# A hybrid decoder step on one core: the sample's attention moved out of the opening into the second half of layer 0

## The reference, cut to what matters

```python
# layer 0 (even)
hp, hs = rms_norm(xp, norm_mix[0]), rms_norm(xs, norm_mix[0])
gate_b, gate_c, xv, q, k, v = split_projection(h, w_in)        # 6 x 512 columns
y_a = gated_short_conv(gate_b, gate_c * xv, conv_w)
# sample: every new token reads its own sequence's cache (8 x 1024 rows of keys
# and of values) at three (window, dilation) pairs, and itself
y_b = combine_branches([dilated_branch_sample(q, k_all, v_all, w, d, wb)
                        for w, d in ((128, 1), (512, 4), (2048, 16))])
x = x + concat([y_a, y_b]) @ w_out
# layer 1 (odd): x = x + pool_mix(rms_norm(x))
# every layer, after its mixer, for prompt and sample:
h = rms_norm(x); q = h @ wq                                    # 8 heads x 2 x 128
expert = top16(top16(q1 @ keys1) + top16(q2 @ keys2))          # of 128 x 128 experts
x = x + sum((softmax(cs) * gelu(h . u_tab[expert])) * v_tab[expert])
```

## Time and profile before

| | us |
|---|---|
| median of three runs | 3018.01 |
| the profiled execution: its own time | 3018.12 |
| its span in the trace | 3016.3 |
| PE busy in the span | 2627.3 (87%) |
| DVE busy | 2088.8 (69%) |
| ACT busy | 1289.9 (43%) |
| POOL busy | 1200.5 (40%) |
| moved by DMA | 1214.94 MB, mean 403 GB/s |
| HBM read / written | 1208.47 MB / 38.37 MB |

### The profile page before, as it was taken

The page is one execution under the profiler, slowest core; times in us unless marked ns, Lnnn a source line. Parts: engine busy times, 40 slices in busy tenths (PEclk is TensorE's granted clock), DMA queues, the critical chain, the costliest instruction groups (busy, mean ns, idle before and its releaser), DMA issues.

```text
span 3016.3 us, 27708 instructions
## 1 busy us (share of the span) xinstructions
PE 2627.3 (87%) x7481; PEld 1297.1 (43%) x7481; DVE 2088.8 (69%) x5117; ACT 1289.9 (43%) x3717; POOL 1200.5 (40%) x1104
## 2 busy tenths in 40 slices
PE   7989999999998887888898988878999977777787
PEld 6665565555544443333444434323444422222222
DVE  3547666787766667777667677777676767677666
ACT  2113445665444344444443444345443444444444
POOL 2103344343444444444444344444434543344442
PEclk9999999999999998999999999999999999999999
DMA  9869999999999999999999999999999999999997
GB/s 353 302 244 371 417 419 416 421 390 395 420 421 422 421 421 391 421 421 404 421 421 421 394 405 422 421 421 389 421 420 420 420 421 414 418 418 415 416 418 325
DMA packets 174472, 1214.94 MB, mean 403 GB/s; under 512 B 19714, under 2 KB 20238, under 8 KB 32613
## 3 DMA queue, kind: packets, MB, share of 16 engines
q0 software_dynamic: 155904, 1124.11, 90.4%
q1 hardware_dynamic: 18413, 89.07, 7.6%
HBM read 1208.47 MB, written 38.37 MB: 413 GB/s over the span
## 4 chain that ended last, share of the span: by engine, by line
DMA 44%; PE 38%; DVE 7%; ACT 6%; issue 3%; POOL 1%; DVEq 0%; SPq 0%; ACTq 0%; POOLq 0%
DMA RING<-in_peer_uv,idx 44%; PE PSUM L1171 24%; PE PSUM L882 10%; DVE RING L1770 4%; ACT diag L1342 2%; ACT L1338 1%; ACT gate L1339 1%; POOL RING L833 1%; PE PSUM L864 1%; ACT L1318 1%; ACT act_h L1338 1%; DVE H L1384 1%; PE PSUM L1162 1%; DMA RING<-in_peer_uv,pidx 1%; PE PSUM L894 0%
## 5 line engine op out<-in xcount | busy, mean ns | idle before, releaser
L1171 PE MATMUL PSUM<-RING,diag 128*128 128x512 f32 (+1 forms) x4160 | 1995.3, 616 | 344.5 <-ACT diag L1342 341.0
L833 POOL DMA_INDIRECT RING<-in_peer_uv,idx x1024 | 1147.7, 1121 | 1610.3 <-PE PSUM L1171 1505.6
L1770 DVE CUSTOM_DVE_ANT_0 RING<-RING,H 128x1024 f32<-128x1024 f32 x1032 | 1264.5, 1226 | 708.1 <-DMA RING<-in_peer_uv,idx 700.2
L1171 PEld LDWEIGHTS PSUM<-RING,diag 128*128 128x128 f32 (+1 forms) x4160 | 750.6, 191 | 1426.5 <-ACT diag L1342 785.1
L1338 ACT ACTIVATE act_h<-dots 128x1 f32<-128x1 f32 x1040 | 207.8, 200 | 1063.1 <-DVE dots L1770 1061.3
L1342 ACT ACTIVATE diag<-ident,gate 128x128 f32<-128x128 f32 x1024 | 411.2, 402 | 39.8 <-PE PSUM L1171 6.6
L882 PE MATMUL PSUM<-HT,WCH 128*128 128x256 f32 (+1 forms) x1536 | 366.4, 384 | 1.3 <-ACT HT L1216 1.3
L882 PEld LDWEIGHTS PSUM<-HT,WCH 128*128 128x128 f32 x1536 | 288.9, 191 | 98.9 <-issue 63.7
L1339 ACT ACTIVATE gate<-act_h,ex 128x1 f32<-128x1 f32 x1024 | 301.6, 294 | 33.2
L1338 ACT ACT_TABLE_LOAD x92 | 118.0, 1283 | 7.6 <-DVE dots L1770 6.0
L1216 ACT ACTIVATE YT<-PSUM 128x264 f32<-128x264 f32 (+2 forms) x68 | 27.0, 398 | 178.0 <-PE PSUM L882 172.4
(11 more groups left out here) (220 smaller groups left out, 1463.4 us busy)
## 6 DMA issues: line engine op xcount, KB each, us to landing
WCH<-in_peer_wq SPq DMA_DIRECT2D x32, 1024.0 KB, 9.2
WCH<-in_w_in_ab SPq DMA_DIRECT2D x18, 1024.0 KB, 9.6
RING<-in_peer_uv,idx POOLq DMA_INDIRECT x1024, 15.0
out_win_k_sample<-in_state_win_k POOLq DMA_DIRECT2D x8, 2016.0 KB, 12.3
out_win_v_sample<-in_state_win_v POOLq DMA_DIRECT2D x8, 2016.0 KB, 10.8
RING<-in_w_in_ab SPq DMA_DIRECT2D x6, 1024.0 KB, 10.9
WCH<-in_w_out_ab SPq DMA_DIRECT2D x6, 1024.0 KB, 9.4
X<-in_x_prompt SPq DMA_DIRECT2D x4, 512.0 KB, 14.8
```

The source lines that it names most:

```text
L833: pool.indirect_dma_start(rows[:, use % SLOTS, :], None, peer_uv.rearrange("l e n -> (l e) n"), bass.IndirectOffsetOnAxis(ap=at, axis=0),) ...
L1171: last = nc.tensor.matmul(PSUM[0:out_n, accumulator(n) + half, :], diag[:, use % DIAGS, 0:out_n], rows[:, use % SLOTS, D + half * 512:D + ...
L1770: V.tensor_tensor_reduce(out=u, in0=u, in1=row, scale=1.0, scalar=0.0, op0=ALU.mult, op1=ALU.add, accum_out=dots[:, tau % SETS, k:k + 1]). ...
```

## The change

The sample's attention, its residual add, its second norm and its queries leave the first half of layer 0 and go to the second. Its projections and its convolution stay in the opening; what is needed later (its query, value and convolution rows) is kept in SBUF tiles that live on.

- `has_sample` is now true for b = 1 in both layers, so the sample's column block rides with `wo`, `wt`, norm 3 and the queries of the second half (264 columns there, 256 in the first).
- The sample's pieces are laid over the second half by position (`sample_pieces`, `threaded`): a sequence's keys every 5 units of width, the softmax, a sequence's values every 4 units. The widths of that half sum to 187 instead of 166, over the same rows 40 to 204. The last four projection chunks go to the attention's steps 13 to 16 instead of 8 to 11.
- Keys and values now come through two buffers, the tile G and the first 1024 columns of YT, not four in RING; keys are multiplied in place. With the space won in RING the opening's weight pairs get seven homes instead of four.
- The value sums are turned round: for each sequence eight matmuls with 128 x 128 value rows as weights and 2 columns moving, into bank 4, instead of two with 512 columns moving; four more bring in the token's own value. `masked` and `gather_heads` go; two copies take their place.
- Jobs use the banks 0 to 3 from the second half on (`cut`), not 0 to 4.
- The last five cache copies start at `wo` chunks 0, 2, 4, 6, 7 of the opening. The expert keys are loaded at `own`, the second half's x rows at `tails`.

```diff
-NW_FIRST = 4
+NW_FIRST = 7
...
-NKV = 4
+NKV = 2
+OWN = 64
+SAMPLE_BANK = 4
...
-NORMS = ((1, 2, 0), (1, 2, 0), (3, 4), (3, 4), (1, 2), (1, 2), (3, 4, 0), (3, 4, 0), (1,), (2,), (3,), (4,), (0,))
+NORMS = ((1, 2, 0), (1, 2), (3, 4), (3, 4, 0), (1, 2), (1, 2), (3, 4, 0), (3, 4, 0), (1,), (2,), (3,), (4,), (0,))
...
 def has_sample(l, b):
-    return (l, b) in ((0, 0), (1, 1))
+    return b == 1
...
+KEYS_AT, KEY_STEP = 14, 5
+SCORED_AT = KEYS_AT + B * KEY_STEP + 1
+WEIGHED_AT = SCORED_AT + 5
+SPREAD_AT = WEIGHED_AT + 7
+SUMS_AT, SUM_STEP = SPREAD_AT + 7, 4
+
+def sample_pieces():
+
+    out = [(6, ("kv", n), 0) for n in range(NKV)]
+    for b in range(B):
+        at = KEYS_AT + b * KEY_STEP
+        out.extend([(at, ("qrep", b), 1), (at + KEY_STEP - 0.5, ("kv", NKV + b), 0)])
+    out.extend([(SCORED_AT, ("scored_sample",), 1), (WEIGHED_AT, ("weighed",), 0), (SPREAD_AT, ("weights",), 1)])
+    for b in range(B):
+        at = SUMS_AT + b * SUM_STEP
+        out.append((at, ("so", b), 1))
+        if B + NKV + b < 2 * B:
+            out.append((at + 1, ("kv", B + NKV + b), 0))
+    out.append((SUMS_AT + (B - 1) * SUM_STEP + 2, ("gathered",), 0))
+    return out
...
-        gated = [("p", b, kind, c) for kind in "cxb" for c in range(CA)]
+        gated = [("p", b, kind, c) for kind in "cx" for c in range(CA)]
+        gated += [None] * (BT * NH + 1 - 3 * CA) + [("p", b, "b", c) for c in range(CA)]
...
+        out = threaded(out, sample_pieces())
...
-    cut = names.index(("hT", 3, 0, 0))
+    cut = names.index(("gain", 2, 0))
...
+        kv = [rows.rearrange("p (t n) -> p t n", t=2) for rows in (G[:, :], YTf[:, 0:2 * DA])]
...
-                    + [("so", 2), ("so", 5), ("so", 7), ("wo", 0, 1), ("wo", 0, 4)])
+                    + [("wo", 0, c) for c in (0, 2, 4, 6, 7)])
...
             def sample_output(b):
...
+                    for c in range(CA):
+                        nc.tensor.matmul(out[:, c, :, :], v_row[:, c * P:(c + 1) * P], own_mix[:, c, :, :],
+                                         start=(c == 0), stop=False, skip_group_check=True)
                 pe.wait_ge(kv_loaded[n % NKV], 48 * (n // NKV + 1))
-                for c in range(2):
-                    last = nc.tensor.matmul(PSUM[0:B * NH, 7, :], SPT[:, c, b, :], kv[:, n % NKV, c, :],
-                                            start=(b == 0 and c == 0), stop=(b == B - 1 and c == 1))
+                for c in range(CA):
+                    heads = slice(b * NH + 2 * c, b * NH + 2 * c + 2)
+                    for t in range(2):
+                        last = nc.tensor.matmul(out[:, c, b, :], kv[n % NKV][:, t, c * P:(c + 1) * P], SPT[:, t, heads],
+                                                start=False, stop=(t == 1), skip_group_check=True)
                 last.then_inc(so_done, 1)
```

More of the change, by code:

```diff
@@ L87, in has_sample, with threaded @@
 def has_sample(l, b):
-    return (l, b) in ((0, 0), (1, 1))
+    return b == 1
 REPEATED = ((1, 0), (1, 1))
-OUTPUTS_AT = {9: (0,), 10: (1, 2), 11: (3, 4), 12: (5,), 13: (6,), 14: (7,)}
+KEYS_AT, KEY_STEP = 14, 5
[16 more added lines that the diff above has]
+    return out
+def threaded(main, among):
+    out, at, left = [], 0.0, sorted(among, key=lambda entry: entry[0])
+    for piece, n in main:
+        while left and left[0][0] <= at:
+            out.append(left.pop(0)[1:])
+        out.append((piece, n))
+        at += n
+    assert not left
+    return out
 def whole_pieces(l, b):
@@ L136, in whole_pieces @@
             if m == 8:
-                out.append((("scored_sample",), 1))
                 out.append((("tails", b), 1))
@@ L141, in whole_pieces @@
             out.append((("count", b, m + 1), 0.9))
-            if m < 8:
-                out.append((("qrep", m), 1))
-            elif m == 8:
-                out.append((("weighed",), 0))
-            else:
-                if m == 9:
-                    out.append((("weights",), 1))
-                for n in OUTPUTS_AT.get(m, ()):
-                    out.append((("so", n), 1))
-                if m == BT * NH - 1:
-                    out.append((("masked",), 1))
-                if m == BT * NH:
-                    out.append((("gathered",), 1))
         for c in range(KD):
@@ L157, in whole_pieces @@
             if c in (4, KD - 1):
-                for j in (*range(BT), "s"):
+                for j in range(BT):
                     out.append((("wt", b, j, c // 7), 1))
@@ L183, in whole_pieces @@
                 out.append((("wt", b, j, half), 1))
-            if b == 0:
-                out.append((("wt", b, "s", half), 1))
+            out.append((("wt", b, "s", half), 1))
+        out = threaded(out, sample_pieces())
     else:
@@ L483, in build @@
         o += 2 * CA * B
-        times = RING[0:B * NH, o:o + NS]
-        o += NS
         own_scores = RING[0:B, o:o + NH]
         o += NH
-        own_column = RING[0:B, o:o + B * NH]
-        o += B * NH
-        by_sample = RING[0:B * NH, o:o + B]
-        o += B
-        own_probs = RING[0:B * NH, o:o + NH]
-        o += NH
         assert o <= SLOTS * ROW
+        sel = X[OWN:OWN + B, 0, :].rearrange("p (b n) -> p b n", b=B)
+        q_row, v_row = (H[OWN:OWN + B, n * DA:(n + 1) * DA] for n in range(2))
         UW = BN + 2
@@ L531, in build @@
         o += NS
+        times = SC[0:B * NH, o:o + NS]
+        o += NS
+        own_column = SC[0:B, o:o + B * NH]
+        own_mix = SC[OWN:OWN + B, o:o + B * NH].rearrange("p (c b h) -> p c b h", c=CA, b=B)
+        o += B * NH
+        by_sample = SC[0:B * NH, o:o + B]
+        o += B
+        own_probs = SC[0:B * NH, o:o + NH]
+        o += NH
+        SPT = SC[:, o:o + 2 * B * NH].rearrange("p (t n) -> p t n", t=2)
+        o += 2 * B * NH
+        ys_kept = SC[:, o:o + CA * B].rearrange("p (c b) -> p c b", c=CA)
+        o += CA * B
         assert o <= T * HC * NK
```

149 lines of the change are left out of this document (58 added, 91 removed).

## The result

| | before | changed |
|---|---|---|
| median of the runs, us | 3018.5 (3016.9 to 3024.6, 4 runs) | 3048.0 (3045.5 to 3049.2, 4 runs) |
| ratio | 1 | 1.0086 (1.0073 to 1.0100) |
| profiled execution, us | 3018.1 | 3049.2 |
| its span, us; mean granted clock | 3016.3; 0.976 | 3047.2; 0.965 |

The change costs 30 us. Forecast were 8 us gained, and a range up to 3024.

The account below looks back on a forecast made before the run. PE's order bounds the opening, the DMA ceiling of 421 GB/s the gathers, and both nearly meet in the second half, with PE leading. 3018.1 - 35 (opening) - 1 (rows 0 to 40) + 28 (half) = 3010 us; range 2998 to 3024.

Parts of the forecast that it names:

- Opening, -35: Up to the first gather: PE's path loses 38.8 us, some given back, net 35 (30 to 40); first gather at 200.5.
- Rows 0 to 40, -1: First 40 rows of gathers: PE loses the sample's scores and 8 columns, DMA nothing, at 418 of 421; 1 us gained.
- Value sums, 0.161 us a record: Second half, on PE: 136 records at 0.161 us each, 21.9 us; low end 0.105 us each, 14.3.
- The half, +28: Rows 40 to 204: PE 483 us, bytes 473, 10 us of idle time left; 493 instead of 465 (ends +20, +34).
- Loads at 421 GB/s: Second half, on the queues: 16 sequences' loads of 0.5 MB, 8.4 MB, are 20 us at 421.
- bytes rival: Second half grows only by its 20 us of loads, PE's idle time taking the rest; total 3002, chance 0.15.
- Four banks, 0: Second half: four banks instead of five cost 0; if PE had to wait for a bank, all rows behind it would.
- the only rival that lengthened the half beyond work and bytes: Second half: late value rows stop PE once landing exceeds 21 us; at 24.8, total 3033; chance 0.12.
- It does not do what it says: Opening gives nothing because something other than PE's path holds the first gather, the half still pays; 3046, chance 0.03.
- signs of "wrong": PE waits for G or YT loads, first gather after 207, half growing by 20 or less, or by over 40.
- PE busy some 97% from there to row 204: Sign of "right": PE's busy share from the first gather, at about 200, to row 204.
- Value-sum records 0.11 us apart: Sign of "right" in the second half: value-sum records 0.11 to 0.16 apart.

Follow-up runs that it names:

- thin loads: Changed kernel with 14 of the sample's 16 key and value loads cut to 3 x 8 KB; 1.0033 of before.
- five banks: Changed kernel with five PSUM banks instead of four until the sample's softmax (row 101 or so); 1.0054 of before.
- late root: Changed kernel with each norm's square root three rows later in ScalarE's list; 1.0051 of before.
- early norm: Changed kernel with VectorE's part of the norm of row 41 issued without its three rows of delay, later norms' square roots three rows later; 1.0064 of before.
- thin weights: Changed kernel with five query weight pairs loaded in rows 0 to 40 cut from 1 MB to 128 KB; 1.0056 of before.
- the kernel before with more bytes: Kernel before with 22 unused loads of 256 KB (5.8 MB) added in rows 0 to 38; 1.0051 of before.

## Why the prediction was wrong

In the profiled executions the opening gave 23 us, rows 0 to 40 gave 7, the half cost 63 and the rest gave 2: 31 us more, where the sum was -35 - 1 + 28. Of the miss, 35 us stand in the half and 12 in the opening; the other two places did better than their terms.

**Opening, -35: the work right, the waits wrong.** PE's work fell by 29.7 us to row 0, and the terms for it came to 31.7: 28.7 for the sample's four kinds of matmuls, 1.0 for narrower chunks and an estimate of 2. The step that failed is the one that added waits, 5.9 us, as gone: by the list of PE's waits the opening had 17.8 us from 60 to 235 and has 16.3 from 60 to 212. Waits of PE for the softmax took their place, as its list shows before and changed:

```profile
PE PSUM L864 <- DVE den L1535: 2.2, 2, 1.8
```

```profile
PE PSUM L871 <- DVE den L1538: 7.2, 12, 2.6
```

The sample's pieces had stood between the attention steps and had hidden that round; I had counted this for the last three sums only. The first gather came at 212.7 instead of 200.5. Fourteen kernels here have the changed opening, with row 0 at 214.5 to 222.5 us, median 218, against 247.3 for the four with the old one: 29 us is its usual gain, and the execution shown lost some 4 more to the clock, which PE had at its lower level for 30.7 us between 60 and 212 (20.5 before).

**Rows 0 to 40, -1.** They gave 7 us. This step hid the cause of the loss: "DMA nothing, and it is at 418 of 421". True before, but there PE was the slower of the two by a little and VectorE built up 10 us of lead. With PE 5 us faster, the ceiling of 421 GB/s became the bound. I priced that only in time, not in the lead. That bytes there take the lead is shown in both kernels; that PE's 5 us did it here is argued.

**Value sums, 0.161 us a record.** They took 0.113: sixteen of them lie between 582.19 and 584.00.

```profile
582.19 1.95 PE L980 MATMUL PSUM<-SC,G 128*128 128x2 f32 x16
584.00 5.38 PE L1174 MATMUL PSUM<-RING,diag 128*128 128x512 f32 x8
```

The Trainium skill's 107 ns for the load of the weights (TensorE: Matmul & The Clock Gate, "LDWEIGHTS (loading the stationary operand)") was the better guess here; the 113 ns from record to record agree with it within 6 ns. The work added in the half was 26 us, below my range of 27 to 34.

**The half, +28.** "With PE more clearly the bound some of it fills" is the step that failed. It came to +63: 26 work, 19 idle, 18 clock. By busy time, the measure that I had used, PE is idle for 32 of the 528 us where I put 10; before it was 16. Idle time of an engine in its order is not slack that more work fills. It was made of waits for the rows' own data, and what made these come later lengthened them: the added bytes did so in two tests, the key pieces hardly. By the experiments on the half's length: bytes of the sample 10 us, bytes of rows 0 to 40 6, banks 5 to 9, the root at row 197 5, sums 12. Each of these has its share of idle time, clock or work in it, and they do not add up to 63.

**Loads at 421 GB/s.** By the time of their queue's packets the 8.4 MB went at 324 GB/s, 26 us of the engines instead of 20; by the rows at the ceiling it would be 376 GB/s and 22 us. The bytes rival was thus nearer than it seemed in its cause, but it forecast a gain: both limits bound, in turn, rather than the longer one.

**Four banks, 0.** The sentence behind it held: PE had to wait for a bank, once, 4.02 us.

**The rivals.** No wait of PE for the sample's loads is in the trace, though some landed after 16 us. That was the only rival that lengthened the half beyond work and bytes; none let idle time or lost clock grow. That 3048 lies beside the 3046 of "It does not do what it says" is chance: the opening did give 23 us here.

**What would show it.** Two of the signs of "wrong" came true, a first gather after 207 and a half that grows by over 40. "PE busy some 97% from there to row 204" came out at 94%. Value-sum records 0.11 us apart, under 410 GB/s in the half and nothing moved after it came true as well, so these told nothing of the idle time.

**What stays open.** The low clock is not fully traced. Four of its seven stretches in rows 40 to 205, 31 of the 51 us, begin in a wait of 4 to 8 us. Three of these went in the kernel that took or shortened the wait: at row 88 with thin loads, at row 101 with five banks, at row 197 with the late root. At row 43 it is less clear: 6.8 us at the lower level stay in the early norm, where the longest wait is down to 2.7 us, and 3.4 with thin weights. The stretch at 625 us, among the value sums, is 13.7 us long here and 3.4 to 13.7 in the other changed kernels near that place, also where three quarters of the sums are left out (3.4 to 10.2). The kernels with the old half have 3.4 us there at most; what brings it was not separated. Nor is the rest of the half's idle time, some 14 us that stay when all the parts tested are thin or mended. The places of the sample's pieces in the order and the two buffers instead of four were not varied.

## What to carry over

Before moving work beside a stretch of gathers, ask what keeps the producer ahead of the consumer there. A lead of some rows is a buffer that pays for every fixed delay in the lists, and it is gone when the stretch just before reaches the transfer ceiling; the busy shares of rows 0 to 40, 98% for PE and 1.01 for the DMA engines in both kernels, did not show it. Look at the queue's share of the engines before pricing moved bytes at the ceiling, and count a wait as gone only if nothing of its kind stands behind it.

## What the runs showed of the hardware

A wait of PE can cost some of its clock too: in the kernel before with more bytes, 6.2 us more idle time in rows 40 to 50 came with 3.6 us lost at the lower clock. The loss does not follow the idle time: in the same rows 10.2 us idle came with 1.6 lost in the changed kernel, 8.6 with 3.7 with five banks and 4.7 with 2.7 with the early norm. The granted clock of the changed kernel was at its lower level, 1.2 GHz, for 51 us of rows 40 to 205 (3.4 before), 10.2 of them from 492.0 on, at the end of the 5.04-us wait. The same 128x512 accumulation averages 623 ns over that stretch against 598. The Trainium skill says (TensorE: Matmul & The Clock Gate, "HAM oscillation — how this bites in real kernels") that PE falls back to its lower clock over waits for loads in the midst of a kernel. The trace agrees for the four stretches that begin in a wait of 4 to 8 us; the longest, 13.7 us at 625, begins in a wait of only 2.2. In all, the lower clock made 18 of the 63 us.

By the time of their packets, loads of 2 KB rows out of a cache went at 324 GB/s in the half and 376 in rows 0 to 40, beside gathers of 8 KB rows at 394 in that half and 414 in those rows. And a wait need not be a pure loss: over the 8 us at row 43 the lead rose from 3.7 to 8.5 us, and taking half of the wait away gained 4.4 us up to row 60 and lost 4.0 of it again up to row 100.
